# Index products in fours over four PSUM banks, with the gate rows, the recurrence's constants and the value copies at other places

## What is computed

```python
h = rms_norm(x, norm_mix[l])
(m_qk, m_v, m_o, m_i, m_f, r_x, r_g, a_q, a_k, a_v, a_qi, a_ki, a_w, gates) = jnp.split(h @ w_in[l], split_at, axis=-1)
m_qk = jax.nn.silu(causal_dwconv(m_qk, mlstm_conv_w[l], mlstm_conv_b[l]))
# branch 1: mLSTM over m_q, m_k, m_v with the gates m_i, m_f
# branch 2: r_x convolved, then the real-gated recurrence h_t = a_t h_(t-1) + sqrt(1-a_t^2) (i_t x_t),
#           a_t = sigmoid(lam)^(8 r_t); softplus(-lam) is its constant per channel
# branch 3: attention of 8 heads whose keys an indexer selects:
logits = jnp.einsum('bqhd,bsd->bqhs', qib, k_idx) * (64 ** -0.5)
score = jnp.einsum('bqh,bqhs->bqs', wb * (8 ** -0.5), jax.nn.relu(logits))
score = jnp.where(visible, score, -jnp.inf)
_, idx = lax.top_k(score, 128)
```

## Time and profile before

| what | value |
|---|---|
| median of three runs | 3539.13 us |
| the profiled execution, its own time | 3542.02 us |
| its span | 3540.2 us |
| TensorE busy | 3495.1 us, 99% |
| VectorE busy | 2166.9 us, 61% |
| ScalarE busy | 1354.4 us, 38% |
| mean granted clock of TensorE | 0.995 of full |
| DMA | 103 GB/s on the mean |
| index products (L1373) | 96 records, 69.7 to 1105.4 us |

### The profile page before, as it was taken

The page is one execution under the profiler, slowest core; times in us unless marked ns, Lnnn a source line. Parts: engine busy times, 40 slices in busy tenths (PEclk is TensorE's granted clock), DMA queues, the critical chain, the costliest instruction groups (busy, mean ns, idle before and its releaser), DMA issues.

```text
span 3540.2 us, 52855 instructions
## 1 busy us (share of the span) xinstructions
PE 3495.1 (99%) x21472; PEld 2858.2 (81%) x21472; DVE 2166.9 (61%) x3052; ACT 1354.4 (38%) x1576; POOL 0.2 (0%) x4
## 2 busy tenths in 40 slices
PE   8999999999999999999999999999999999999998
PEld 6778778888877787888888778888888778888887
DVE  6887667876388876687763666652233577652233
ACT  6465433322274644333222343232222343332223
POOL 0000000000000000000000000000000000000000
PEclk9999999999999999999999999999999999999999
DMA  4222224553233222345532340123222330133221
GB/s 131 84 81 60 83 96 157 178 197 130 85 99 93 68 64 72 121 143 190 196 123 86 94 131 26 60 98 107 95 95 86 94 130 27 64 114 98 95 95 71
DMA packets 273310, 364.46 MB, mean 103 GB/s; under 512 B 22636, under 2 KB 218976, under 8 KB 271840
## 3 DMA queue, kind: packets, MB, share of 16 engines
q1 hardware_dynamic: 247856, 311.34, 27.5%
q10 hardware_dynamic: 25264, 50.43, 4.1%
HBM read 351.79 MB, written 9.96 MB: 102 GB/s over the span
## 4 chain that ended last, share of the span: by engine, by line
PE 92%; DVE 4%; DVEq 2%; ACT 1%; issue 1%; DMA 0%; ACTq 0%; SPq 0%
PE banks L248 26%; PE banks L250 26%; PE banks L249 26%; PE banks L3193 1%; PE banks L3209 1%; PE banks L3137 1%; PE banks L3086 1%; PE banks L2095 1%; PE banks L2121 1%; PE banks L2138 1%; PE banks L1388 1%; DVE arena L1769 1%; DVE w_lo L170 0%; PE banks L587 0%; PE banks L588 0%
## 5 line engine op out<-in xcount | busy, mean ns | idle before, releaser
L248 PE MATMUL banks<-act_hi,w_hi 128*128 128x512 f32 x4064 | 1606.6, 395 | 6.3 <-DVE act_lo L533 1.6
L250 PE MATMUL banks<-act_hi,w_lo 128*128 128x512 f32 x4064 | 1584.0, 390 | 0.0
L249 PE MATMUL banks<-act_lo,w_hi 128*128 128x512 f32 x4064 | 1582.9, 390 | 0.0
L170 DVE TENSOR_TENSOR w_lo<-w_raw,w_hi 128x2048 fp32r<-128x2048 f32 (+1 forms) x280 | 629.2, 2247 | 609.2 <-ACT w_hi L164 605.2
L248 PEld LDWEIGHTS banks<-act_hi,w_hi 128*128 128x128 f32 x4064 | 763.0, 188 | 199.1 <-issue 33.4
L250 PEld LDWEIGHTS banks<-act_hi,w_lo 128*128 128x128 f32 x4064 | 762.3, 188 | 162.2
L249 PEld LDWEIGHTS banks<-act_lo,w_hi 128*128 128x128 f32 x4064 | 762.9, 188 | 158.5 <-issue 3.8
L164 ACT ACTIVATE w_hi<-w_raw 128x2048 fp32r<-128x2048 f32 (+1 forms) x280 | 526.6, 1881 | 936.1 <-PE banks L250 870.6
L2305 DVE SCALAR_TENSOR_TENSOR arena<-arena,small 128x512 f32<-128x512 f32 x168 | 126.3, 752 | 13.2 <-issue 0.4
L248 PE MATMUL banks<-w_hi,act_hi 128*128 128x256 f32 x384 | 110.2, 287 | 0.4 <-DVE w_lo L170 0.4
L249 PE MATMUL banks<-w_lo,act_hi 128*128 128x256 f32 x384 | 108.6, 283 | 0.0
(11 more groups left out here) (408 smaller groups left out, 3337.2 us busy)
## 6 DMA issues: line engine op xcount, KB each, us to landing
w_raw<-in_w_in SPq DMA_DIRECT2D x98, 1024.0 KB, 5.4
arena<-in_ada_w ACTq DMA_DIRECT2D x24, 2048.0 KB, 8.1
w_raw<-in_ffn_up SPq DMA_DIRECT2D x48, 1024.0 KB, 5.2
w_raw<-in_w_gu SPq DMA_DIRECT2D x44, 1024.0 KB, 5.1
w_raw<-in_ffn_down SPq DMA_DIRECT2D x24, 1024.0 KB, 5.0
w_raw<-in_w_down SPq DMA_DIRECT2D x20, 1024.0 KB, 4.9
w_raw<-in_w_out SPq DMA_DIRECT2D x16, 1024.0 KB, 5.0
w_raw<-in_w_branch SPq DMA_DIRECT2D x12, 1024.0 KB, 5.1
```

Source lines behind the costliest of these rows:

```text
L170: self.core.nc.vector.tensor_tensor(view(self.lo[:, s]), view(self.raw[:, s]), view(self.hi[:, s]).bitcast(FP32), ALU.subtract)\
L248: nc.tensor.matmul(out, wh, ah, start=first, stop=False)
L249: nc.tensor.matmul(out, wh, al, start=False, stop=False)
L250: return nc.tensor.matmul(out, wl, ah, start=False, stop=last)
```

## The change

- Index products in fours: nothing behind the first and third tile of a section, four heads behind the second and fourth; product c goes into bank 4 + c % 4, and waits for the relu four before it. In query block 3, heads 0 and 1 wait for the first index query tile, all later ones for the last. ScalarE's relus and VectorE's sums are moved likewise.
- The gate rows are transposed further on: in layer 0 behind the first tile of aqk + 1 (was: second of aqk), in layer 1 behind the first of mqk (was: third of aqk + 1), each after a wait for all relus so far, since bank 6 is now one of the four. The product that uses bank 6 next waits for the copy. VectorE's copy and ScalarE's Exp move with it.
- `lru_constants` moves on VectorE from behind the first tile of aqk + 1 to behind the first convolution of mqk + 1.
- The copies of the value banks 0 and 1 wait for the second token tile of the second half, not for the fourth.

```diff
@@ index_pe @@
-                if c >= 2:
-                    pe.wait_ge(relu_ok, c - 1)
-                if c == 0 and raw:
-                    pe.wait_ge(n.x, 7)
+                if c >= 4:
+                    pe.wait_ge(relu_ok, c - 3)
+                elif c == 0 and raw:
+                    pe.wait_ge(n.x, 8)
                 if qt == ST - 1:
-                    pe.wait_ge(turn_used, 4 + h // 2)
+                    pe.wait_ge(turn_used, 4 + h // 2 if h < 2 else 7)
+                if c == (18 if late else 10):
+                    pe.wait_ge(am_ok, 1)
-                nc.tensor.matmul(ps[:, 4 + c % 2, 0:w], A[rows, self.QI + h // 2, qt * P:qt * P + P],
+                nc.tensor.matmul(ps[:, 4 + c % 4, 0:w], A[rows, self.QI + h // 2, qt * P:qt * P + P],
@@ pe_part @@
                 self.dense_tile(pe, u["aqk"], b, n.lo if late and b == 0 else None)
-                if b == 1 and not late:
-                    am_pe(pe)
-                index_pe(pe, 3, (2 * b, 2 * b + 1))
+                if b % 2:
+                    index_pe(pe, 3, range(2 * b - 2, 2 * b + 2))
             for b in range(4):
                 self.dense_tile(pe, u["aqk"] + 1, b)
-                if b == 2 and late:
+                if b == 0 and not late:
+                    pe.wait_ge(relu_ok, 8)
                     am_pe(pe)
-                index_pe(pe, 2, (2 * b, 2 * b + 1))
+                if b % 2:
+                    index_pe(pe, 2, range(2 * b - 2, 2 * b + 2))
             for b in range(4):
                 self.dense_tile(pe, u["mqk"], b)
-                index_pe(pe, 1, (2 * b, 2 * b + 1))
+                if b == 0 and late:
+                    pe.wait_ge(relu_ok, 16)
+                    am_pe(pe)
+                if b % 2:
+                    index_pe(pe, 1, range(2 * b - 2, 2 * b + 2))
@@ act_part @@
-                index_act(act, 3 - i // 4, (i % 4 * 2, i % 4 * 2 + 1))
-                if i == 2 and not late:
+                if i % 2:
+                    index_act(act, 3 - i // 4, range(i % 4 * 2 - 2, i % 4 * 2 + 2))
+                if i == 5 and not late:
                     enm_act(act)
-            if late:
-                enm_act(act)
...
+                if i == 2 and late:
+                    enm_act(act)
             for b in range(4):
-                self.wait_tile(act, u["mv"], 3)
+                self.wait_tile(act, u["mv"], 2 if b < 2 else 3)
@@ dve_part @@
-                if b == 1 and not late:
-                    am_dve(dve)
-                index_sum(dve, 3, (2 * b, 2 * b + 1))
+                if b % 2:
+                    index_sum(dve, 3, range(2 * b - 2, 2 * b + 2))
...
-                if b == 3 and late:
+                if b == 0 and not late:
                     am_dve(dve)
-                index_sum(dve, 2, (2 * b, 2 * b + 1))
-                if b == 0:
-                    lru_constants(dve)
+                if b % 2:
+                    index_sum(dve, 2, range(2 * b - 2, 2 * b + 2))
                 self.top_rounds(dve, 3, b, b + 1)
             for b in range(4):
                 conv_dve(dve, b + 1, b, "mconv", b, A[:, self.MQ + b, :], 4, b)
+                if b == 0 and late:
+                    am_dve(dve)
...
                 conv_dve(dve, b + 5, b, "mconv", b + 4, A[:, self.MK + b, :], 4, b + 4)
+                if b == 0:
+                    lru_constants(dve)
                 if b % 2:
                     self.schedule.lo(dve, u["mqk"] + 2, b // 2)
```

More of the change, by code:

```diff
@@ L1519, in index_act @@
                     act.wait_ge(relu_used, c - 1)
-                nc.scalar.activation(relu[c % 2][:, 0:w], ps[:, 4 + c % 2, 0:w], ACT.Relu,
+                nc.scalar.activation(relu[c % 2][:, 0:w], ps[:, 4 + c % 4, 0:w], ACT.Relu,
                                      scale=64 ** -0.5).then_inc(relu_ok, 1)
@@ L1630, in act_part @@
                     self.schedule.hi(act, um + 1, b // 2)
-                if i <= 4:
-                    index_act(act, 1, (2 * b, 2 * b + 1))
+                if i in (2, 4):
+                    index_act(act, 1, range(2 * b - 2, 2 * b + 2))
+                if i == 2 and late:
+                    enm_act(act)
                 if i >= 2:
@@ L1956, in dve_part @@
                 conv_dve(dve, b + 1, b, "mconv", b, A[:, self.MQ + b, :], 4, b)
+                if b == 0 and late:
+                    am_dve(dve)
                 if b % 2:
                     self.schedule.lo(dve, u["mqk"] + 1, b // 2)
-                index_sum(dve, 1, (2 * b, 2 * b + 1))
+                if b % 2:
+                    index_sum(dve, 1, range(2 * b - 2, 2 * b + 2))
                 self.top_rounds(dve, 3, 4 + b, 5 + b)
```

## The result

| kernel | median | runs | ratio to before, 95% interval |
|---|---|---|---|
| before | 3539.46 us | 3537.78 to 3541.58, 7 | |
| changed | 3551.56 us | 3548.60 to 3553.08, 7 | 1.0031 (1.0022 to 1.0040) |

The change makes the kernel 12.1 us slower, a third of a per cent, and the interval leaves out 1. The forecast was 3548.6 us, 9.5 slower, with a range from 3538.5 to 3554.

The account below looks back on a forecast made before the run. VectorE was taken to set the pace in the second half of the index-product stretch. Layer 0 at +4.0 us and layer 1 at +5.5 made +9.5 on 3539.1, so 3548.6 us, range 3538.5 to 3554.

Parts of the forecast that it names:

- The bound: Index products of layer 0: the chain leaves TensorE at 129.92 us and VectorE sets the pace in the second half.
- The switches: Index products on TensorE: a four costs 0.44 us less than two pairs, 2.6 us per layer, 5.3 in all.
- VectorE's idle time, layer 0: Ahead of the values' weight rest VectorE idles 11.3 us against 8.2, so that rest ends 3.1 us later.
- Layer 1: VectorE's idle time ahead of the values' weight rest grows from 1.1 to 6.5 us; the rest ends 5.4 us later.
- The clock: Lower TensorE clock after the waits at the values: 1.7 us lost in layer 0, 0.85 us in layer 1.
- fourth rival: More clock is lost: waits in both layers each leave 6.6 us at half clock; 3552.9 us, chance 0.12.
- first rival: VectorE's lateness ahead of the values governs: 3548.6 us, own range 3544.5 to 3552, chance 0.62.
- The values: Early copies of value banks 0 and 1 remove the 0.78 us wait at rx's first tile: 0.8 us per layer.
- The second: TensorE keeps its saving in switches, values and a stall: -9.9 us, 3529.2 us, chance 0.11.
- The third: VectorE's idle time does not grow and the values' half starts as before: about 3540 us, chance 0.15.

## Why the prediction was right, step by step

**The bound.** Right. The prediction's first step, that the second half of the stretch runs at VectorE's pace, carried all the others.

**The switches.** In the changed kernel a four costs 77.30 - 74.73 = 2.57 us between the last L250 and the second step behind it. Less two steps (0.45) that is 2.12, where two pairs cost 2 x 1.27 = 2.53 by the earlier trace rows: 0.42 us saved, 0.44 forecast. The eight records take 76.97 - 75.05 = 1.92 us, as forecast. The second pair of a four does not pay the price of entry. TensorE did save about 2.5 us per layer (2.4 by the landmarks of the run with fours in layer 0 only), and spent them waiting.

**VectorE's idle time, layer 0.** Forecast 11.3 us against 8.2, measured 11.2. VectorE's waits in the changed kernel from 72.7 to 175 us, then from 1032.6 to 1140:

```profile
DVE arena L1712 <- ACT arena L1516: 11.2, 6, 2.9
...
DVE arena L1712 <- ACT arena L1516: 6.9, 3, 5.4
DVE arena L1774 <- ACTq L1535: 1.6, 2, 1.3
```

The values came 3.34 us later (forecast 3.1), with a wait of 5.91 us (forecast 5.3). The piece that the constants had filled shows as the longest but one: the timeline has 2.78 us ahead of the second key tile (forecast 2.7).

**Layer 1.** The waits were forecast at 3.1, 3 to 4 and 2 us and came at 2.91, 3.32 and 3.05. The 5.2 us of VectorE behind the forget gate measured 5.37. The step that was mis-sized is the sum of its idle time, forecast to grow by 5.4 us, from 1.1 to 6.5. The rows above with the 0.4 us of its own issue make 8.9, but 0.45 of it is a wait for a turned copy at its start, which the window of the earlier trace rows leaves out (the changed kernel is 4.7 us later there). Like for like it is 8.4 us against 1.4, 7.0 more. Most of the difference is 1.6 us ahead of the convolutions (L1774), for which I had 0.3: the longer of its two waits (1.25 us) is for a tile that TensorE made late at half clock after the transposes. I had called such a drop absorbed, since TensorE has slack there; but VectorE has none, and waits for TensorE's tiles in its turn. So the values came 6.55 us later in place of 5.4; the rest ended 6.8 later, but TensorE had come 0.2 us after it before.

**The clock.** The term that was most off. Forecast 1.7 us in layer 0 and 0.85 in layer 1; measured +2.46 and +2.69 from the values' first half to the first score, where the work is the same. The windows of the changed kernel after the two waits and, third, after the 2.9 us wait:

```profile
169.74:175.70 5.96, 5.96 (x29) 5.96 (x30) 5.51 (x9) 1.71 (x3) 0.00 (x0) 0.53 0.59 179
...
1138.30:1145.10 6.80, 6.27 (x30) 6.27 (x31) 6.36 (x10) 2.55 (x3) 0.00 (x0) 0.53 0.52 154
1070.00:1073.40 3.40, 3.40 (x10) 2.65 (x10) 2.38 (x4) 3.30 (x7) 0.00 (x0) 0.55 0.31 111
```

At both waits at the values the clock stood at 1.2 GHz for 6.8 us, not 3.4 (granted clock 0.50 from 168.6 to 175.3 and from 1138.0 to 1144.7 us), the first part of it inside the wait. So the term came out as in the fourth rival of the prediction (more clock is lost), on top of the first. The two clock terms are 2.6 us over the forecast, the values 1.15 over in layer 1 and 0.24 in layer 0, and the value copies gained 0.39 more: 3.6 us, which makes the 9.5 into the 13.05 of the profile. The medians, 12.1, lie 2.6 us over the forecast. That is inside the first rival's own range and only 1.3 us under the fourth's figure; the time alone could not have told the two apart.

**The values.** 1.0 us per layer, 0.8 forecast. By starts, the step from the last matmul of the values into rx was 193.99 - 192.93 = 1.06 us before and is 198.72 - 198.60 = 0.12 now; the 0.78 of the row counts only from the modelled end of that matmul.

**The rivals.** The second (TensorE keeps its saving) needed VectorE's idle time to fall below 6 us; it rose to 11.2. The Trainium skill's rule that a change of tiling mode drains the engine ("TensorEngine Tiling (Array Packing)", "Key Properties") agrees with the 0.42 us saved per four, though the trace shows only a price at the switch and not what the engine does in it; the kernel got slower all the same. The third needed VectorE's idle time to stay as it was, and it grew in both layers.

## What to carry to other kernels

Before moving work on an engine's queue, add up that engine's work and idle time ahead of the next thing that others wait for: a move that stays on the same side of that point gives nothing unless idle time shrinks, and here the right place was the first gap behind it, which took 12 us off the changed kernel. Look also at whether a wait that such a move makes is followed by a drop of the clock: with the constants alone moved, that was most of the cost. Grouping the products of a busy TensorE saves its switches, but it also groups their readers, and these stood in front of copies that a third engine waited for. A stall costs more than its length when the clock falls behind it (2.5 and 2.7 us more here).

## What the runs showed of the hardware that I had not expected

One and the same wait does not always bring the same clock. In two kernels with the same code up to that point, TensorE waits 1.39 us at the transposes of layer 0; the kernel with the forget gate first then runs at half clock, the one with fours in layer 0 only does not. The window right behind it, of the former (in the latter the granted clock is 1.00 over the same window):

```profile
97.68:101.09 3.41, 3.41 (x9) 2.73 (x9) 2.17 (x5) 1.74 (x3) 0.00 (x0) 0.51 1.04 336
```

I had taken 1.57 us without a drop and 2.06 with one for a border between the two; there is none that one trace could give. At the first recurrence product ten waits of 1.57 us in five kernels brought no drop, and of eight of 1.82 to 1.85 us two did (in layer 1 of the kernel with the fours and the constants in the gap, and of the one with the forget gate first). How long the drop lasts is not fixed by the wait either: behind the same 2.9 us at the first four of 384 columns it was 3.4 us in the changed kernel and 6.8 in the two that differ from it only in the place of the constants. A forecast needs a chance for each wait of over a microsecond, and the profiled executions of one kernel can differ by some us for this alone.
